# Differential attention: where in a head's three parts the next head's keys are rotated

## The reference, cut to what matters

```
q = apply_rope(q, cos, sin)
k = apply_rope(k, cos, sin)
k_all = jnp.concatenate([k, kc], axis=1)
v_all = jnp.concatenate([v, vc], axis=1)
...
o1 = sweep_attention(qq[..., 0, :], kk[..., 0, :], vv)
o2 = sweep_attention(qq[..., 1, :], kk[..., 1, :], vv)
o = o1 - lam.astype(o1.dtype) * o2
o = rms_norm(o, subln_g) * (1.0 - lam_init)
```

## Time and profile before

| what | value |
|---|---|
| median of 3 runs | 1320.11 us (1317.59 to 1322.25) |
| the profiled execution | 1316.09 us, span 1314.3 us |
| PE, PEld, DVE, ACT, POOL busy | 92%, 83%, 62%, 44%, 6% of the span |
| mean granted TensorE clock | 0.97 |
| the differential attention's heads | about 806 to 1057 us of the span |

### The profile page before, as it was taken

The page is one execution under the profiler, slowest core; times in us unless marked ns, Lnnn a source line. Parts: engine busy times, 40 slices in busy tenths (PEclk is TensorE's granted clock), DMA queues, the critical chain, the costliest instruction groups (busy, mean ns, idle before and its releaser), DMA issues. The chain is left out here.

```text
span 1314.3 us, 22878 instructions
## 1 busy us (share of the span) xinstructions
PE 1211.0 (92%) x8638; PEld 1090.5 (83%) x8638; DVE 808.6 (62%) x1607; ACT 583.2 (44%) x1066; POOL 82.4 (6%) x92
## 2 busy tenths in 40 slices
PE   5989999988997998999999988999999989998985
PEld 5989899978997997988898877788777779887775
DVE  4765655547986755565565534656566667675754
ACT  4754444443222342434243434555554545564543
POOL 1320000002231000000000000000000000001000
PEclk9999999989998999999999989999999989889998
DMA  7544444433322552478876751122111124322110
GB/s 268 179 147 162 139 148 145 143 112 113 128 67 96 164 178 81 145 274 302 285 261 223 262 204 49 64 81 64 49 64 49 64 67 143 112 70 76 65 49 33
DMA packets 48061, 175.04 MB, mean 133 GB/s; under 512 B 5392, under 2 KB 5520, under 8 KB 47568
## 3 DMA queue, kind: packets, MB, share of 16 engines
q1 hardware_dynamic: 47088, 168.92, 37.9%
q0 software_dynamic: 864, 4.65, 0.9%
HBM read 172.50 MB, written 1.05 MB: 132 GB/s over the span
## 5 line engine op out<-in xcount | busy, mean ns | idle before, releaser
L1688 DVE TENSOR_TENSOR w_lo<-w_raw,w_hi 128x1024 fp32r<-128x1024 f32 (+1 forms) x272 | 331.0, 1223 | 209.0 <-ACT w_hi L1487 171.2
L1487 ACT CAST w_hi<-w_raw 128x1024 fp32r<-128x1024 f32 (+1 forms) x272 | 274.7, 1035 | 82.8 <-PE lin L1193 51.8
L1191 PE MATMUL lin<-XH,w_hi 128*128 128x256 f32 x448 | 129.5, 289 | 14.3 <-DVE w_lo L1688 14.3
L1192 PE MATMUL lin<-XL,w_hi 128*128 128x256 f32 x448 | 127.3, 284 | 0.0
L1193 PE MATMUL lin<-XH,w_lo 128*128 128x256 f32 x448 | 127.2, 284 | 0.0
L1191 PE MATMUL lin<-NH,w_hi 128*128 128x256 f32 x416 | 120.4, 289 | 1.3 <-DVE NL L1832 1.3
L1192 PE MATMUL lin<-NL,w_hi 128*128 128x256 f32 x416 | 117.6, 283 | 0.0
L1193 PE MATMUL lin<-NH,w_lo 128*128 128x256 f32 x416 | 117.5, 283 | 0.0
L1619 ACT ACTIVATE probs<-score,stat 128x512 f32<-128x512 f32 (+1 forms) x88 | 53.0, 607 | 116.9 <-DVE stat L1955 87.3
L1191 PEld LDWEIGHTS lin<-XH,w_hi 128*128 128x128 f32 x448 | 86.4, 193 | 17.1 <-ACT w_hi L1487 13.6
L1423 POOL TENSOR_TENSOR ms<-ms,mhalf 128x4 f32<-128x4 f32 (+1 forms) x26 | 29.3, 1125 | 1037.2 <-DVE ms L1814 1037.2
(11 more groups left out here) (375 smaller groups left out, 3177.1 us busy)
## 6 DMA issues: line engine op xcount, KB each, us to landing
w_raw<-in_ada SPq DMA_DIRECT2D x48, 512.0 KB, 5.4
w_raw<-in_w_out SPq DMA_DIRECT2D x32, 512.0 KB, 3.3
w_raw<-in_gate SPq DMA_DIRECT2D x22, 512.0 KB, 6.1
w_raw<-in_up SPq DMA_DIRECT2D x22, 512.0 KB, 3.7
w_raw<-in_ffn_out SPq DMA_DIRECT2D x16, 512.0 KB, 3.9
w_raw<-in_q SPq DMA_DIRECT2D x16, 512.0 KB, 3.8
w_raw<-in_z SPq DMA_DIRECT2D x16, 512.0 KB, 3.3
w_raw<-in_k SPq DMA_DIRECT2D x10, 512.0 KB, 3.3
```

The source lines that it names most:

```text
L1191: nc.tensor.matmul(bank[:, 0:W], wh, moving(H, kk), start=first, stop=False)
L1192: nc.tensor.matmul(bank[:, 0:W], wh, moving(L, kk), start=False, stop=False)
L1487: scal.copy(w_hi[:, i % HL, 0:n], raw[:, tile["i"] % RAW, 0:n]).then_inc(w_hi_ready, 1)
L1688: vec.tensor_sub(w_lo[:, i % HL, 0:n], raw[:, tile["i"] % RAW, 0:n], w_hi[:, i % HL, 0:n].bitcast(F32)).then_inc(w_lo_ready, 1)
```

## The change

The rotation of the next head's keys, and the note of how many rotations its scores need, move from the fill of part 0 to the front of the projection branch in the fill of part 1. Nothing is added or removed.

```
             if part == 0 and nxt < DA_HEADS:
                 rope_2(Q2, nxt)
                 wide_2("k_2", nxt, K2)
+            elif part == 1 and nxt < DA_HEADS:
                 rope_2(K2, nxt)
                 roped_2.append(n_rope[0])
-            elif part == 1 and nxt < DA_HEADS:
                 if h < 3:
                     values_2(2 * h + 2)
```

## The result

The changed kernel takes 1333.93 us (median of 4 runs, 1331.17 to 1336.09), the kernel before 1318.85 (4 runs, 1317.28 to 1322.25; one more run than the three shown ahead of the prediction). The ratio is 1.0125 with a 95% interval of 1.0105 to 1.0144. The forecast was 1324.9 us in a range of 1320.7 to 1331.0: the direction was right, the size was not, and the time lies outside the range. The medians are 15.1 us apart where 4.8 were forecast.

What follows compares the result with a forecast made beforehand. PE was taken to set the pace; 3.1 us of longer waits in four heads plus 1.7 us for one clock fall made 4.8 us, giving 1324.9 us in terms of the runs' median, range 1320.7 to 1331.0.

Steps and rivals of the forecast that it cites:

- What bounds the stage, and which heads matter: In the heads PE sets the pace; heads 0 to 2 neither gain nor lose, heads 3 to 6 lose 3.1 us.
- The exponentials come 2.55 us earlier: In head 4, part 2's exponentials end at 962.55 in place of 965.10, 7.70 us after PE begins the norm factor.
- The rotation's wait, 0.77 us a head: Behind part 1's transposes in heads 3 to 6, PE waits for the moved rotation: 0.77 us a head, 3.1 us together.
- The clock: Behind the longer waits in heads 3 to 6, PE's clock falls to half once, costing 1.7 us.
- the seven waits: PE waits of 1.99 to 2.66 us across the trace, taken as entered at full clock; three had falls behind them.
- four long ones, 13.8 us: Upper bound on the clock term in heads 3 to 6: four long falls, 13.8 us.
- rival 2: Falls behind three or four waits in heads 3 to 6: 10.0 us, 1330.1 us (8.3 with three); chance 0.13.
- Rival 3: Rotation done in the transposes' shadow, PE no longer waits in heads 3 to 6: 7.2 us gained, 1312.9; chance 0.06.

Runs made afterwards that it cites:

- e3_first3: Kernel before with the rotation's move made in heads 0 to 2 alone: 1320.70 us, ratio 1.0011.
- e9_sums_behind: Changed kernel with the light sums of squares moved behind the dense projection in part 2 of heads 3 to 6: 1326.95 us, ratio 1.0077 to the kernel before.
- e8_busy3: Changed kernel with three dense products on PE ahead of the next head's score products in heads 3 to 6: 1331.24 us, ratio 1.0102 to the kernel before.
- e6_late2: Kernel before with one idle 128x1024 copy on ACT ahead of part 2's exponentials in heads 3 to 6: 1333.40 us, ratio 1.0108.
- e7_late3: Kernel before with two idle copies, 128x1024 and 128x512, on ACT ahead of part 2's exponentials in heads 3 to 6: 1338.88 us, ratio 1.0160.
- e1_split: Kernel before with only DVE's three rotation products moved to part 1, ACT's four copies staying in part 0: 1309.79 us, ratio 0.9937.
- e5_late1: Kernel before with one idle 128x512 copy on ACT ahead of part 2's exponentials in heads 3 to 6: 1323.99 us, ratio 1.0045.
- e4_head4: Kernel before with the rotation's move made in head 4 alone: 1327.08 us, ratio 1.0060.

## Why the prediction was wrong

- **What bounds the stage, and which heads matter**: right. The change costs heads 0 to 2 nothing (head 2 takes 31.89 us, and e3_first3); the four heads with a gate projection carry 16.8 of the 17.7 us.
- **The exponentials come 2.55 us earlier**: right, 7.70 us behind the norm factor as in head 7.
- **The rotation's wait, 0.77 us a head**: right in kind, a third too small. It is 1.10: the square holds ACT 0.66 us ahead of the copies, not the 0.52 ahead of a CAST (0.14); the handover from DVE to PE takes 972.32 - 971.77 - 0.42 = 0.13, not 0.05 (0.08); and the sums follow the released products by 941.49 - 940.32 = 1.17, not 1.06 (0.11). The sum of the waits is 4.4 us, not 3.1.
- **The clock**: this is the step that failed, the term "one fall: 1.7 us". There were four falls, and three of them lasted two or three times as long as the one that I priced: 13.7 us of full speed in place of 1.7. Both factors were too small. *The number*: three falls behind seven waits give 1.7 falls for four waits, and not the one that I counted. And waits of 2 us and more were the wrong sample. The trace of the kernel before has eleven stretches of half clock between 70 and 1165 us; three of them come with the seven waits, the other eight have only shorter waits ahead of them. One stands right behind the heads, behind a wait of 1.44 us, sums of squares and the products of a norm factor (PE's rows, and its clock behind them):

```profile
1058.44 1.05 PE L1294 MATMUL sum_bank<-ones,sqr 128*128 128x2 f32 x8 [1.44 <-ACT sqr L1529]
1059.79 1.13 PE L1305 MATMUL sum_bank<-ident,ms 128*128 128x128 f32 x8 [0.30 <-issue]
1061.00:1068.00 7.00, 5.09 (x22) 0.51 0.24 75
```

*The price*: it was taken at the shorter of the two rows that I had. The fall behind the wait of 1.99 us, which ends at 777.10, was the longest of all, half clock from 778 to 794 and on, and I did not price it:

```profile
778.00:794.00 16.00, 10.92 (x43) 0.50 0.05 20
```

What sets whether and for how long the clock falls stays open in part. e9_sums_behind shows that moving the light sums away from the wait halves the full speed lost. But the kind of work behind a wait doesn't sort the seven waits: four were followed at once by projections, and two of these fell; of the other three one did. The wait of 2.60 us in head 0, with a projection and score products ahead of it and score products and a projection behind, was followed by a fall in 2 of the 12 profiles (the changed kernel and e8_busy3), the waits of 2.16 to 2.97 us in heads 3 to 6 of the changed kernel, e6_late2 and e7_late3 in 12 of 12. Whether it also matters at which moment a wait comes, no run varied by itself.

- **The bound** of "four long ones, 13.8 us" was met almost exactly, but by luck: the four lost 3.4, 3.4, 1.7 and 5.1 us, not 3.4 each, and with the longest fall of the trace before as the price it would have been more than twice as high. It was left out of the range all the same.
- **The rivals**: rival 2, falls behind three or four waits, is what happened; it had 0.13 and was priced at 10.0, with short falls, where the stage shows 16.8. The prediction read against the change what the section "HAM oscillation — how this bites in real kernels" of the Trainium skill's page "TensorE: Matmul & The Clock Gate" says of waits in a loop, a drop of the clock at each tile. The waits of that example are for DMA and some 3 to 5 us long, so it gave no ground for falls behind waits of 2.5; this trace shows a drop in each of the four heads all the same, behind waits of 2.97 us. Rival 3 fails for this change but is right for e1_split, to its very number (7.2 us).
- One slip that changes nothing: the wait of 2.66 us ends at 791.28, within that long stretch of half clock, so the seven waits entered at full clock reach from 1.99 to 2.62 us.
- I should have asked what stands around the wait, not only how long others had been. Also, the kernel before had little to spare at this place: 0.5 us more brought the first falls (e5_late1).

## What to carry to other kernels

Price a new wait of TensorE in two parts: the wait, and what the clock does behind it. Where such waits stand among light work, as here among transposes, score products and sums of two columns, take a fall behind each of them as the likely case; how far the light work ahead of the wait counts, no run here varied. Collect the falls of the whole trace, also those behind short waits, before putting a chance on a new one. And when a step is shared by two engines, its halves can be moved apart: here DVE's products belonged behind the maxima, ACT's copies did not.

## What was not expected of the hardware

- With light work around it, a TensorE wait of 1.60 us in place of 1.08 was enough for falls behind two of four (e5_late1); at 2.16, 2.69 and 2.97 us it was four of four (e6_late2, e7_late3, the changed kernel), and at 2.97 with the sums moved away three of four (e9_sums_behind), each in one profile.
- A fall in heads 3 to 6 cost between 1.7 and 5.1 us of full speed, though in the changed kernel PE began its projection 2 to 4 us behind the wait.
- Nine dense products whose result nobody uses, in the wait, made the changed kernel faster by some 10 us (ratios of 1.0045 and 1.0125 to the kernel before; the two were measured in different sessions).
- An ordinary wait of 1.08 us was followed by a fall in the head behind a long one (e4_head4), and in none of the 13 other cases in four profiles.
